# Between the sublayers of a ten-sublayer block: halves of rows split straight from the transposes' bank, the norm weight as a broadcast row, and the next weight pieces split between the norm's steps

## The reference

```python
def rms_norm(x, gain=None):
    xf = x.astype(jnp.float32)
    y = xf * lax.rsqrt(jnp.mean(xf * xf, axis=-1, keepdims=True) + EPS)
    if gain is not None:
        y = y * gain.astype(jnp.float32)
    return y.astype(x.dtype)
...
        h = rms_norm(x, ffn1_norms[l, 0])
        x = x + 0.5 * rms_norm(swiglu(h, ffn1_w13[l], ffn1_w2[l]), ffn1_norms[l, 1])
        h = rms_norm(x, mix_norms[l, 0])
```

## Time and profile before

| | us |
|---|---|
| median of 3 runs | 2397.11 |
| lowest, highest | 2395.66, 2397.49 |
| the profiled execution's own time | 2396.83 |
| its span in the trace | 2395.0 |

### The profile page before, as it was taken

One profiled execution on the slowest core, in us unless ns is written; L12 is line 12 of the kernel. 1 busy time (PEld: TensorE's weight loads), 2 busy tenths in 40 slices (PEclk: granted clock), 3 DMA queues, 4 the chain that ended last, 5 costly groups with the idle time before them and its releaser, 6 DMA issues.

```text
span 2395.0 us, 29682 instructions
## 1 busy us (share of the span) xinstructions
PE 2184.4 (91%) x12707; PEld 1912.9 (80%) x12707; DVE 1402.5 (59%) x1697; ACT 1020.5 (43%) x1334; POOL 99.9 (4%) x111
## 2 busy tenths in 40 slices
PE   6989897889888999799989999989989998898998
PEld 5878786878777899678768879979977877787997
DVE  4656765646775645555676465455455566655554
ACT  4444443434443433344535344344433444443432
POOL 0100100100010000000000000000000000000000
PEclk9989998989899999899999999999999999999999
DMA  6343233343233555334435355545544354442652
GB/s 242 116 152 108 87 123 114 125 161 124 71 106 124 173 188 182 133 106 159 142 132 203 107 182 185 185 161 182 187 141 145 109 168 154 150 159 97 211 193 89
DMA packets 190971, 351.59 MB, mean 147 GB/s; under 512 B 8124, under 2 KB 84984, under 8 KB 190840
## 3 DMA queue, kind: packets, MB, share of 16 engines
q1 hardware_dynamic: 189400, 344.46, 42.4%
q0 software_dynamic: 1440, 5.24, 0.7%
HBM read 348.63 MB, written 1.05 MB: 146 GB/s over the span
## 4 chain that ended last, share of the span: by engine, by line
PE 76%; DVE 14%; ACT 5%; issue 3%; DMA 1%; POOL 1%; SPq 0%; POOLq 0%; DVEq 0%; ACTq 0%
PE bank L1786 14%; PE bank L1780 14%; PE bank L1776 14%; PE bank L1806 7%; PE bank L1803 7%; PE bank L1800 7%; DVE raw_r L2236 4%; PE bank L1824 3%; PE bank L1944 2%; PE bank L1841 2%; PE bank L1815 2%; PE bank L1862 1%; POOL stat L2703 1%; ACT high L2049 1%; DVE units L2330 1%
## 5 line engine op out<-in xcount | busy, mean ns | idle before, releaser
L2236 DVE TENSOR_TENSOR raw_r<-raw,high 128x2048 fp32r<-128x2048 f32 (+1 forms) x314 | 709.5, 2278 | 110.0 <-ACT high L2049 110.0
L1776 PE MATMUL bank<-high,units_r 128*128 128x512 f32 (+1 forms) x1696 | 689.1, 406 | 38.9 <-ACT units_r L2066 17.6
L2049 ACT ACTIVATE high<-raw 128x2048 fp32r<-128x2048 f32 (+1 forms) x314 | 591.0, 1894 | 264.9 <-PE bank L1786 229.5
L1780 PE MATMUL bank<-high,units_r 128*128 128x512 f32 (+1 forms) x1696 | 674.8, 398 | 12.2 <-DVE units_r L2253 12.0
L1786 PE MATMUL bank<-raw_r,units_r 128*128 128x512 f32 (+1 forms) x1696 | 463.3, 396 | 39.6 <-DVE raw_r L2236 39.5
L1776 PEld LDWEIGHTS bank<-high,units_r 128*128 128x128 f32 x1696 | 327.0, 193 | 110.2 <-issue 34.0
L1786 PEld LDWEIGHTS bank<-raw_r,units_r 128*128 128x128 f32 x1696 | 324.2, 192 | 111.4 <-DVE raw_r L2236 43.6
L1800 PE MATMUL bank<-units_r,high 128*128 128x256 f32 x1600 | 401.8, 287 | 0.0
L1803 PE MATMUL bank<-units_r,high 128*128 128x256 f32 x1600 | 398.3, 285 | 0.0
L1780 PEld LDWEIGHTS bank<-high,units_r 128*128 128x128 f32 x1696 | 326.9, 193 | 82.6 <-DVE units_r L2253 18.5
L1800 PEld LDWEIGHTS bank<-units_r,high 128*128 128x128 f32 x1600 | 309.9, 194 | 1.3
(11 more groups left out here) (228 smaller groups left out, 1782.8 us busy)
## 6 DMA issues: line engine op xcount, KB each, us to landing
raw<-in_ffn_w_dram SPq DMA_DIRECT2D x132, 1024.0 KB, 5.0
raw<-in_w_in_dram SPq DMA_DIRECT2D x108, 1024.0 KB, 5.0
raw<-in_w_out_dram SPq DMA_DIRECT2D x24, 1024.0 KB, 4.9
raw<-in_cross_wkv_dram SPq DMA_DIRECT2D x16, 1024.0 KB, 5.1
raw<-in_w_branch_dram SPq DMA_DIRECT2D x12, 1024.0 KB, 4.7
raw<-in_cross_wq_dram SPq DMA_DIRECT2D x8, 1024.0 KB, 5.1
raw<-in_cross_wo_dram SPq DMA_DIRECT2D x8, 1024.0 KB, 4.9
raw<-in_w_in_dram SPq DMA_DIRECT2D x4, 832.0 KB, 4.3
```

Of the source, the lines that this page charges most:

```text
L1776: pe.matmul(o, h.high(k0 + k)[:, span], w[:, k, :], start=start and k == 0, stop=False, skip_group_check=True)
L1780: pe.matmul(o, h.low(k0 + k)[:, span], w[:, k, :], start=False, stop=False, skip_group_check=True)
L2049: act.activation(high, p.raw, ACT.Copy).then_inc(*mark(s.whigh, ("whigh", p.i)))
L2236: dve.tensor_tensor(low, p.raw, high.bitcast(F32), ALU.subtract).then_inc(*mark(s.wlow, ("wlow", p.i)))
```

## The change

It does four things.

1. Post: the weight is multiplied in before the mean is known. DVE writes bank times `gpost` into a unit `yg` while ACT squares the other bank (each waits for the other to leave its bank), and after the rstd one DVE operation of 1024 columns, (yg x rstd) + x, gives x.
2. The pre weight no longer multiplies the transposed rows. It is a broadcast row `gpre` (a new 128 x 1024 tile, filled by one POOL DMA in each seam but the last, ten in all), and the norm's last step is (x x rstd) x gpre in one DVE operation. Every transposed tile that is to be split is split from its bank: ACT's high part and DVE's low part read PSUM, and the copy or product ahead of them is gone, here and in all other places with such a split (100 in all; 8 with a weight per channel become four ACT and four DVE operations each). The bank is released after the low part.
3. `Seam.steps` yields between its steps, and the splits of next pieces are put there: in `tail` piece A (and B where the tail has four pieces) between the steps of t = 0, in `begin` two more between the steps of t = 1, each with its low part right behind. In the first seam all four pieces are split ahead of row 1's norm. Mixing to cross has them for t = 0 only.
4. There are 25 units instead of 26.

The core of the diff, with the parts left out that only rename:

```diff
+    def turn_pairs(self, name, src, need, h, t, scal=None, gains=None):
+
+        banks = [self.B.take() for _ in h.pairs]
+        for q, bank in enumerate(banks):
+            self.work += 512
+            self.do("turn", name=name, q=q, src=src, need=need, bank=bank)
+        for q, bank in enumerate(banks):
+            self.split_bank(name, q, bank, h.pairs[q], t, ("turnp", name, q), scal,
+                            None if gains is None else gains[:, 4 * q:4 * q + 4])
+            h.made(t, q, name)
+
+    def split_bank(self, name, q, bank, pair, t, need, scal=None, gains=None):
+        self.do("turn_split", name=name, q=q, bank=bank, pair=pair, t=t, need=need, scal=scal, gains=gains)
+        self.B.give(bank, ("low", name, q))
...
+    def steps(self, t):
+        plan, name, nn = self.plan, f"{self.name}.x{t}", f"{self.name}.n{t}"
+        x = plan.xt[t].ap
         if self.yb:
-            tmp = plan.U.take()
+            yg, junk = plan.U.take(), plan.U.take()
             ss, s1 = plan.st(2), plan.st(1)
-            plan.do("post", name=name, need=[("prod", self.name, t)], banks=self.yb[t], tmp=tmp, ss=ss, s1=s1,
-                    f=4.0 if self.half else 1.0, gain=("gpost", self.name), x=plan.xt[t].ap, old=plan.x_made[t])
+            plan.do("post_squares", name=name, need=[("prod", self.name, t)], banks=self.yb[t], junk=junk, ss=ss, yg=yg,
+                    gain=("gpost", self.name))
             for b in self.yb[t]:
-                plan.B.give(b, ("posted", name))
-            plan.gp_used = ("posted", name)
-            plan.U.give(tmp, ("x", name))
+                plan.B.give(b, ("posted", name), ("squares", name))
+            plan.gpost_used = ("posted", name)
+            plan.U.give(junk, ("squares", name))
+            yield
+            plan.do("post_mean", name=name, ss=ss, s1=s1, f=4.0 if self.half else 1.0)
+            yield
+            plan.do("post_x", name=name, yg=yg, s1=s1, x=x, old=plan.x_made[t])
+            plan.U.give(yg, ("x", name))
             plan.x_made[t] = ("x", name)
         if self.norm:
-            self.row[t] = plan.norm_a(f"{self.name}.n{t}", plan.xt[t].ap, [plan.x_made[t]])
+            tmp, ss = plan.U.take(), plan.st(1)
+            plan.do("norm_squares", name=nn, src=x, need=[plan.x_made[t]], tmp=tmp, ss=ss)
+            yield
+            plan.do("norm_mean", name=nn, ss=ss)
+            yield
+            plan.do("norm_scale", name=nn, src=x, tmp=tmp, ss=ss, gain=("gpre", self.name))
+            plan.gpre_used = ("row", nn)
+            self.row[t] = tmp
+
+    def turn(self, t, between=()):
+        between = list(between)
+        for _ in self.steps(t):
+            if between:
+                between.pop(0)()
+        for part in between:
+            part()
         if t:
-            plan.hold = False
-            plan.pump()
+            self.plan.hold = False
+            self.plan.pump()
...
+    toks = []
     for t in range(2):
         for wi, (w, k0, h) in enumerate(ws):
-            if before and (t, wi) in before:
-                before[t, wi]()
             for pi, (kk0, p) in enumerate(w):
                 end = wi == len(ws) - 1 and pi == len(w) - 1
-                if t and end and seam.norm:
-                    seam.turn_row0()
-                if t:
-                    plan.hold = end
-                plan.tok(seam.name, p, t, seam.yb[t], h, k0 + kk0, first and wi == 0 and pi == 0, end)
-        if t == 0:
-            if before and "mid" in before:
-                before["mid"]()
-            seam.turn(0)
+                toks.append((t, wi if pi == 0 else None, p, h, k0 + kk0, first and wi == 0 and pi == 0, end))
+    half = len(toks) // 2
+
+    def put(t, wi, p, h, k0, start, end):
+        if before and (t, wi) in before:
+            before[t, wi]()
+        plan.tok(seam.name, p, t, seam.yb[t], h, k0, start, end)
+
+    for tok in toks[:half]:
+        put(*tok)
+    if before and "mid" in before:
+        before["mid"]()
+    plan.hold = True
+    steps = seam.steps(0)
+    next(steps, None)
+    for tok in toks[half:-1]:
+        put(*tok)
+        next(steps, None)
+        if tok is not toks[half]:
+            plan.split_next(True)
+            next(steps, None)
+            plan.low_next()
+    for _ in steps:
+        plan.low_next()
+    if seam.norm:
+        seam.turn_row(0)
+    put(*toks[-1])
 
 
 def begin(plan, seam, make_jobs):
     if seam.h is None:
-        seam.turn_row0()
-    seam.turn(1)
-    jobs = make_jobs()
-    yield from plan.mm_halves(jobs, seam.h, seam.turn_row1)
+        seam.turn_row(0)
+    jobs = None
+    if seam.yb is None:
+        plan.pump()
+        jobs = make_jobs()
+    seam.turn(1, [lambda: plan.split_next(True), plan.low_next, lambda: plan.split_next(True), plan.low_next])
+    jobs = jobs or make_jobs()
+    yield from plan.mm_halves(jobs, seam.h, lambda: seam.turn_row(1))
...
+    def turn_split(name, q, bank, pair, t, need, scal, gains, **_):
         hi, lo = pair
-        hold.wait_ge(*at(need))
-        for n in hi.after:
-            hold.wait_ge(*at(n))
-        act.activation(seen(hi.r, t), seen(lo.ap, t), ACT.Copy).then_inc(*mark(s.ahigh, ("high", name, q)))
+        for n in (need, *hi.after):
+            hold.wait_ge(*at(n))
+        if scal is not None or gains is not None:
+            hold.wait_ge(*at(("gT",)))
+        if gains is None:
+            high = act.activation(seen(hi.r, t), quad(bank.ap), ACT.Copy, scale=1.0 if scal is None else scal)
+        else:
+            for k in range(4):
+                high = act.activation(seen(hi.r, t)[:, k, :], quad(bank.ap)[:, k, :], ACT.Copy, scale=gains[:, k:k + 1])
+        high.then_inc(*mark(s.ahigh, ("high", name, q)))
...
-    def turn_split(name, q, pair, t, **_):
+            dve.tensor_copy(seen(dst.ap, t), quad(bank.ap)).then_inc(*mark(s.vout, ("turned", name, q)))
+
+    def turn_split(name, q, bank, pair, t, scal, gains, **_):
         hi, lo = pair
         hold.wait_ge(*at(("high", name, q)))
-        dve.tensor_tensor(seen(lo.r, t), seen(lo.ap, t), seen(hi.r, t).bitcast(F32), ALU.subtract).then_inc(
-            *mark(s.alow, ("low", name, q)))
+        for n in lo.after:
+            hold.wait_ge(*at(n))
+        if gains is not None:
+            for k in range(4):
+                low = dve.scalar_tensor_tensor(out=seen(lo.r, t)[:, k, :], in0=quad(bank.ap)[:, k, :],
+                                               scalar=gains[:, k:k + 1], in1=seen(hi.r, t)[:, k, :].bitcast(F32),
+                                               op0=ALU.mult, op1=ALU.subtract)
+        elif scal is not None:
+            low = dve.scalar_tensor_tensor(out=seen(lo.r, t), in0=quad(bank.ap), scalar=scal,
+                                           in1=seen(hi.r, t).bitcast(F32), op0=ALU.mult, op1=ALU.subtract)
+        else:
+            low = dve.tensor_tensor(seen(lo.r, t), quad(bank.ap), seen(hi.r, t).bitcast(F32), ALU.subtract)
+        low.then_inc(*mark(s.alow, ("low", name, q)))
...
+    def norm_scale(name, src, tmp, ss, gain, **_):
         hold.wait_ge(*at(("rstd", name)))
-        dve.tensor_scalar(tmp.ap, src, ss, None, ALU.mult).then_inc(*mark(s.vout, ("row", name)))
-
-    def post(name, banks, tmp, ss, s1, f, gain, x, old, **_):
+        if gain is None:
+            dve.tensor_scalar(tmp.ap, src, ss, None, ALU.mult).then_inc(*mark(s.vout, ("row", name)))
+        else:
+            hold.wait_ge(*at(gain))
+            dve.scalar_tensor_tensor(out=tmp.ap, in0=src, scalar=ss, in1=m.gpre[:, :], op0=ALU.mult,
+                                     op1=ALU.mult).then_inc(*mark(s.vout, ("row", name)))
+
+    def post_squares(name, need, banks, yg, gain, **_):
+        for n in (*need, *yg.after):
+            hold.wait_ge(*at(n))
+        hold.wait_ge(*at(gain))
+        dve.tensor_tensor(yg.ap[:, 512:], banks[1].ap, m.gpost[:, 512:], ALU.mult).then_inc(
+            *mark(s.vout, ("posted_1", name)))
+        hold.wait_ge(*at(("squares_0", name)))
+        dve.tensor_tensor(yg.ap[:, 0:512], banks[0].ap, m.gpost[:, 0:512], ALU.mult).then_inc(
+            *mark(s.vout, ("posted", name)))
+
+    def post_mean(name, ss, s1, f, **_):
         hold.wait_ge(*at(("squares", name)))
         dve.tensor_tensor(s1, ss[:, 0:1], ss[:, 1:2], ALU.add).then_inc(*mark(s.vstep))
         hold.wait_ge(*last(s.vstep))
         dve.tensor_scalar(s1, s1, f / DM, f * EPS, ALU.mult, ALU.add).then_inc(*mark(s.vstat, ("mean", name)))
+
+    def post_x(name, yg, s1, x, old, **_):
         hold.wait_ge(*at(("rstd", name)))
-        hold.wait_ge(*at(gain))
-        for c in range(2):
-            sl = slice(c * 512, c * 512 + 512)
-            dve.scalar_tensor_tensor(out=tmp.ap[:, sl], in0=banks[c].ap, scalar=s1, in1=m.gpost[:, sl], op0=ALU.mult,
-                                     op1=ALU.mult).then_inc(*mark(s.vout, *([("posted", name)] if c else [])))
-        hold.wait_ge(*last(s.vout))
+        hold.wait_ge(*at(("posted", name)))
```

(3 more changed lines are left out.)

151 lines of the change are left out of this document (70 added, 81 removed).

## The result

| | before | changed |
|---|---|---|
| median, us | 2396.39 | 2419.23 |
| lowest, highest | 2395.08 to 2397.49 | 2417.15 to 2419.91 |
| profiled execution's span | 2395.0 | 2418.1 |
| ratio, 95% interval | | 1.0094 [1.0077, 1.0112] |

The change costs 22.8 us. It was forecast as +28.5, for the most part in the same places.

The account below looks back on a forecast made before the run. PE, busy 91% of the span, was taken as the bound, the seams' stretches ending with the post and norm chain plus one low part; 36.1 - 3.4 + 2 - 1.2 - 5 = +28.5 us gave 2425, range 2402 to 2444.

Parts of the forecast that it names:

- The mechanism: In the seams' chains, each pair of high and low part adds 3.15 us; row 1 comes at +13.4 with two.
- (b): In the seams, the second half costs nothing, as PE finds everything ready after row 1 and the clock recovers: 2408; chance 0.12.
- (d): In the chains, a pair adds nothing because the low part runs while DVE would idle: faster, 2353; chance 0.07.
- (e): Whole kernel: savings outside the seams reach what the chains lose, no change beyond 4.8 us; chance 0.05.
- Second halves: Behind row 1 in seven seams: C starts later and runs longer at half clock, +2.5 us with two pairs.
- First halves: Row 0 later: +2.4 us in a0.y, +4.0 cross to `ffn2`, +2.5 `ffn2` to `ffn1`, +1.8 `ffn1` to mixing.
- the clock's 1.7: In a0.y's first half, 1.7 us of clock counted before A starts at 391.4, where it started at 389.06.
- Mixing to cross, end: Mixing to cross: row 1's chain has no splits, -3.4 us for two; end: only post, x earlier, -1.2.
- Start: First seam: four pieces' splits ahead of row 1's norm and the new row's transfer, +2 us (0 to +3.5).
- Splits from the bank elsewhere: Outside the seams: about ten waits each lose a copy of 0.59 to 0.69 us, -5 (-7 to -3).
- Rival (c): Attention and feed-forward: one unit less and banks held longer add waits for buffers, ending above 2440; chance 0.06.
- The prediction's threshold: PE's clock in the seams: a loss of 1.5 to 3 us behind waits of 2.4 us or more, none behind shorter.

Follow-up runs that it names:

- experiment 4: Changed kernel with splits put where the chain leaves an engine idle, no weight's low part inside a chain, start in the old order; 2325.58 us.
- Experiment 3: Changed kernel with the splits of weights in the order of the kernel before, the other parts of the change kept; 2366.36 us.
- experiment 11: Kernel before the change with 25 units instead of 26 and nothing else changed; 2397.15 us.
- experiment 8: Changed kernel with weights' splits in the old order, rows split from a copy as before, every copy on its old engine; 2387.44 us.
- experiment 9: Experiment 3 with a turn of ACT and DVE given up for each copy that is gone, so other copies keep their old engines; 2363.87 us.
- experiment 5: experiment 4 with piece C's low part moved between row 1's addition to x and the norm's mean; 2336.41 us.

## Why the prediction was right, point by point

**The mechanism.** Right, and shown by the row of three, two pairs, one and none. A pair adds 3.0 to 3.2 (3.15). The chain alone takes 7.06 (7.1). With two pairs row 1 is at +13.24 (13.4). The wait moved from the low parts to the norm's scale: nine waits of row 0 from 2.5 to 4.9 and seven of row 1 from 6.5 to 7.9. The prediction said 3 to 5 and 7 to 8.5; four of the nine lie below 3 and three of the seven below 7. Rivals (b), (d) and (e) are out. One of its sums doesn't add up: 1.4 for the squares, 1.0 and 1.22 make 3.6, and it has x at +3.8. The traces have x at +3.76 (experiment 4, the seam at 954), since the squares take 1.45 and the operation 1.28.

**Second halves.** The terms of the prediction give +17.2 (its text has 2.5 for a seam with two pairs, its sum 2.4 to 2.6); 15.3 measured.

**First halves.** Right in sum for five seams (+16.4 measured, 14.1 forecast), wrong in a0.y and a1.y: 0.5 instead of 2.4 each. The step that failed is the clock's 1.7 behind the wait for row 0. The wait was there, 2.96 us, yet the transposes behind it took 1.09, the price at full clock, and the granted clock stayed at 1.00:

```profile
388.00:392.00 4.00, 3.23 (x18) 2.81 (x19) 4.00 (x4) 1.09 (x2) 0.00 (x0) 1.00 0.56 210
```

My own bound "+0.7 without the clock's loss" is what came. The prediction names a clock that holds at 1.00 through the waits as a sign of being wrong; for these two waits it held, behind the long ones it did not.

**Mixing to cross, end.** -2.7 and -1.2, forecast -3.4 and -1.2.

**Start.** +4.2, my range ended at 3.5. Experiment 3 has the old order at the start and ends it about 1 us late; with the order of the changed kernel it is 3.3 more. The first 1 us goes with the new row's transfer: PE has the positions, for which it waits, at 15.44 instead of 14.24, though they are issued earlier (at 9.80 instead of 10.23). In all other kernels with this row it has them at 15.1 to 15.7, in experiment 11, without it, at 14.0. I had taken this transfer as shared bandwidth of at most 1.7 us and put 2 in all.

**Splits from the bank elsewhere.** The largest miss: -5 (-7 to -3) forecast, -10.0 seen between the seams, and 23.6 for this part by itself. The failing step is "about ten waits lie outside the seams and each loses a copy", 0.59 to 0.69 each. Between experiments 8 and 9 the waits for rows' high parts alone lose 10.6, most of them 0.66 to 1.0 each and one 1.7; waits under other names lose 4.8 net (those for low parts of weights 3.7, for L2726 1.5, while those for rows' low parts grow by 1.2), and the clock gives 5.6. I had no term for the last two. That a copy also holds up what stands behind it on ACT and DVE would explain the other names; it isn't shown wait by wait. Some of it was lost again in the changed kernel: 5 us with the new post (experiment 8 outside the seams). The price "reading the bank costs nothing" was right. The changed kernel's groups:

```profile
L2313 DVE TENSOR_TENSOR units_r<-bank,units_r 128x512 fp32r<-128x512 f32 x76 | 50.0, 686 | 63.3 <-ACT units_r L2114 63.3
...
L2114 ACT ACTIVATE units_r<-bank 128x512 fp32r<-128x512 f32 x84 | 47.6, 596 | 163.1 <-PE bank L1864 144.7
```

686 and 596 ns against 689 and 632 from SBUF. The Trainium skill's 120 fixed cycles from PSUM against 58 ("VectorE: DVE Perf Modes", "The TRN2 errata — SBUF-src ops pay a fixed extra latency per instruction") would make DVE's an estimated 65 ns longer. The runs contradict it (3 ns shorter), and the measurement decides. Its ScalarE row, 52 cycles less from PSUM, an estimated 43 ns, is near the 36 ns of the traces.

**Rival (c).** It did not come: the time lies below its 2440. One unit less costs nothing in the kernel before (experiment 11), but there post takes one unit, not two. Banks held until the low part is done were not tried alone; with them experiment 9 is still 23.6 us faster than experiment 8. Engines of copies: 2.5 us at most, the prediction had "some 3".

**Luck.** The total is nearer than its terms. Three were forecast too high, by 10.6 us together (a0.y and a1.y, the second halves, all else between the seams), and the others but the end too low, by 5.2 together, so that only 5.4 is left.

## What to carry to other kernels

Before you put work "between the steps" of a chain, ask on each engine who has the gap and how long it is: ACT's gap of 2.4 us between two squares took a 1.9 us high part for nothing, while DVE, which carries the chain, had gaps of 0.66 us and 1.22 us, and every low part of 2.3 us there delayed the row. What the next piece needs can be split before the chain or behind it. And when PE waits for a chain, look for a piece that it can do meanwhile: moving eight transposes behind one more piece of work was worth 18 us beside the kernel that had the best splits. Last, taking out copies was worth more than the waits that bore their name: 23.6 us against 15.1 (experiments 8 and 9).

## What the runs showed of the hardware that I had not expected

The clock does not follow the length of one wait. After 2.96 us idle the transposes took 1.09 (changed kernel, 388.77), after 2.93 they took 1.88 (experiment 5, 392.26), and after 2.02 they took 1.15 but the products behind them 0.63 instead of 0.39 (experiment 4). The prediction's threshold, a loss behind 2.4 us or more and none behind less, holds neither way. It differs even within one run. Experiment 5 has this row in its first seam of cross to `ffn2`, with both products and transposes at the full rate behind it:

```profile
1359.78 1.09 PE L1871 MATMUL bank<-consts,units 128*128 128x128 f32 x8 [2.95 <-DVE units L2392]
1360.63 0.48 PE L1832 MATMUL bank<-high,units_r 128*128 128x512 f32 x1
1360.95 0.39 PE L1836 MATMUL bank<-high,units_r 128*128 128x512 f32 x1
```

What decides between the two is open. The stretch of experiment 4 behind its wait of 2.02:

```profile
392.00:396.00 4.00, 3.91 (x15) 3.27 (x16) 4.00 (x3) 1.09 (x2) 0.00 (x0) 0.62 0.00 0
```
